# Expert weights read as one run per partition, with strided transposes, in a hybrid backbone step on one core

## Chip, core and metric

One NeuronCore of one Trainium2 chip runs the whole program as a single launch. The metric is the device time of one execution in microseconds. Work is spread over TensorE (PE in the rows, with PEld for its loads of the stationary operand), VectorE (DVE), ScalarE (ACT), GpSimd (POOL) and SyncE (SP). DMAs issued by SP travel on queue q1, those of GpSimd on q0 and those of ScalarE on q10; all run on the same 16 DMA engines.

## What is computed

One layer of a backbone over 512 latent and 128 context tokens of width 1024: a token-mixing half (retention, attention, a diagonal state space), then a mixture of 16 experts. The change touches the experts alone:

```python
logits = (h @ w_router) + b_router            # 16 experts in 4 groups, top 2 inside the best group
hid = silu(einsum('bld,edf->blef', h, w_gate)) * einsum('bld,edf->blef', h, w_up)
out = einsum('blef,efd->bld', hid * combine[..., None], w_down)
```

`w_gate` and `w_up` are 16 matrices of 1024 x 512, `w_down` 16 of 512 x 1024, all float32, so each matrix is 2 MB. An expert computes only on the tokens that chose it.

## The kernel before

The program runs in phases. The last one starts with the output projection and the router (lines 977 to 1036), goes on with the experts (1040 to 1112) and ends with a gather of the expert rows, a sum and a final norm.

**Routing.** The 640 tokens are five tiles of 128 rows, `NROWS[:, t, :]`. VectorE ranks the tokens of each expert and the experts by their number of tokens; GpSimd scatters the rows to the slots of their experts in DRAM (`scratch_x`, line 2657, ten indirect DMAs of 128 rows of 4 KB), in two parts of tiles (tiles 0 to 2, then 3 and 4). The first expert's rows don't go that way: `pick` (1020) multiplies 128 columns of `NROWS` as the stationary operand with a matrix of zeros and ones, which gathers and transposes at once; it makes 40 matmuls, in two parts of 24 and 16.

**Tiles of experts.** There are 13 tiles of 128 slots. Four belong to one expert each (S), nine are in three groups of three where the last 32 slots of each tile belong to a fourth expert. For a tile the steps are `rows` (1040: eight transposes of 128 x 128 from `ROWS2` into PSUM, copied to `COLS`, skipped for tile 0), `gate` and `up` (1072: eight contraction steps of 128 over the 1024 inputs), `turn` (1081: four transposes of `HID`, copied to `HIDT`) and `down` (1089: four contraction steps over the 512 hidden columns, two halves of the output). `MOE_STEPS` writes down the order in which TensorE, VectorE and ScalarE take them. A float32 matmul is two passes on TensorE and a transpose is one, and the rows count passes. In a transpose the data is the stationary operand and the identity matrix moves.

**Weights.** SP brings one 2 MB matrix per DMA in the order of `WEIGHTS` into a ring of seven homes (`load_weights`, 1237, its DMA on line 1244). `home_free` (1246) waits until the matmuls that read the home's last content are done; the home of matrix 6 also waits for the scatter and for the store of `NROWS` in `scratch_h2`. From the fourth matrix on SP needs the expert's number (1266), which VectorE has when the ranks are known. The first three matrices are sent between 852 and 884 us, the next from 975 us on.

**Rows of a tile.** GpSimd waits for all ten scatters, then loads the rows of each tile (512 KB, lines 2682 to 2686) into one of two buffers, as soon as the buffer's last rows are transposed. ScalarE stores each tile's result (512 KB).

With `(k p) c -> p k c` a partition p holds rows p, 128 + p, 256 + p and so on of a matrix: eight runs of 2 KB for `w_gate` and `w_up`, four of 4 KB for `w_down`. The contraction step k then needs inputs 128 k to 128 k + 127, which are neighbouring columns of `ROWS2`, `NROWS` and `HID`.

Of the kernel before, what the change touches and what calls it, by code (L numbers as in the profile page):

```python
# [12 lines left out]
P = 128  # L13
D = 1024
KD = D // P
# [31 lines left out]
def build(nc, a, STOP=99):  # L47
# [6 lines left out]
    def sb(name, shape, dt=F32):  # L54
        return ctx.enter_context(nc.sbuf_tensor(name, shape, dt))

    ident = sb("ident", [P, P])
# [185 lines left out]
    PICK = Region(AQK_AT + 2048).take(NT, P)  # L243
    assert r.at == AQK_AT + 2048 + NT * P
    NROWS_AT = r.at
    NROWS = r.take(NT, D)
# [55 lines left out]
    ROWS2 = r.take(2, D)  # L302
# [4 lines left out]
    HID = r.take(3, 512)  # L307
# [7 lines left out]
    RING = len(W_HOME)  # L315
# [18 lines left out]
    banks = ctx.enter_context(nc.psum_tensor("banks", [P, 8, 512], F32))  # L334
# [54 lines left out]
    slot_in = [sem(f"expert_weights_in{j}") for j in range(RING)]  # L389
# [46 lines left out]
    def at_least(eng, s, n):  # L436

        if not isinstance(n, int) or n > 0:
            eng.wait_ge(s, n)
# [171 lines left out]
    def _(pe):  # L611
# [3 lines left out]
        mm = nc.tensor.matmul  # L615
# [231 lines left out]
        for i, (d, t) in enumerate(KV_ORDER):  # L847
# [4 lines left out]
            for h in range(RH):  # L852
                hs = slice(P * h, P * h + P)
                last = mm(out[:, hs], RK[:, t, hs], VZ[:, i % 3, hs], start=True, stop=True)
            vec.close(last)
        pe.wait_ge(kv_done, len(KV_ORDER))
        for t in range(NT):
            ts_ = slice(P * t, P * t + P)
            out = vec.open(pe)
            for h in range(RH):  # L860
                last = mm(out[:, P * h:P * h + P], RKT[:, h, ts_], RQT[:, h, ts_], start=True, stop=True)
# [5 lines left out]
            for h in range(RH):  # L867
                hs = slice(P * h, P * h + P)
                last = mm(out[:, hs], SS[:, t % 2, hs], RV[:, t, hs], start=True, stop=t == NS)
                if t < NS:  # L870
                    for d in range(2):
                        last = mm(out[:, hs], QX[:, t % 2, d, h, :], ST[:, d, t, hs], start=False, stop=d == 1)
# [83 lines left out]
        for n in range(2):  # L956
            for branch, x in enumerate((ROT, ATT, YT)):
# [3 lines left out]
                for t in range(NT):  # L961
                    for chan, w in list(zip(chans, ws))[::-1]:
                        out = chan.open(pe)
                        for k in range(4):
                            last = mm(out, x[:, k, P * t:P * t + P], w[:, k, :], start=k == 0, stop=k == 3)  # L965
# [55 lines left out]
        def pick(part):  # L1021

            lo, hi = ROUTE_PARTS[part]
            pe.wait_ge(picked, part + 1)
            if part == 0:
                for half in range(2):
                    mm(banks[:, 6 + half, :], PICK[:, NT - 1, :], NROWS[:, 0, 0:512], start=True, stop=False)
            for t in range(lo, hi):
                for k in range(KD):
                    last = mm(banks[:, 6 + k // 4, P * (k % 4):P * (k % 4) + P], NROWS[:, t, P * k:P * k + P], PICK[:, t, :],  # L1030
                              start=False, stop=t == NT - 1 and k % 4 == 3)
            if part:
                last.then_inc(row_t, 1)

        steps = dict(out=project_out, turn=turn_rows, logits=logits, rank=rank, pick=pick)
        for step in OUT_STEPS:
            steps[step[0]](*step[1:])
# [3 lines left out]
        def slot_rows(t):  # L1041
            if t == 0:
                return
            pe.wait_ge(row_in[t % 2], 16 * rows_loaded[t])
            at_least(pe, col_d, t)
            at_least(pe, col_a, t)
            for k in range(KD):
                last = nc.tensor.transpose(banks[:, k // 4, P * (k % 4):P * (k % 4) + P], ROWS2[:, t % 2, P * k:P * k + P], ident[:])
            last.then_inc(row_t, 1)

        def expert_weights(which, t):
# [29 lines left out]
        def slot_turn(t):  # L1081
            n = nth["turn", t]
            pe.wait_ge(gu_free, unit_of["up", t] + 1)
            at_least(pe, hid_c, n)
            for k in range(4):
                last = nc.tensor.transpose(banks[:, 4, P * k:P * k + P], HID[:, t % 3, P * k:P * k + P], ident[:])
            last.then_inc(hid_t, 1)

        def slot_down(t):
# [3 lines left out]
            for half, (full, emptied) in enumerate(((dn0, out_d), (dn1, out_a))):  # L1093
                at_least(pe, emptied, n)
                slot_matmuls(banks[:, 5 + half, :], lambda k: HIDT[:, t % 3, P * k:P * k + P], ws, 4,
                             slice(512 * half, 512 * half + 512)).then_inc(full, 1)

        steps = dict(rows=slot_rows, gate=lambda t: gate_or_up("gate", t), up=lambda t: gate_or_up("up", t), turn=slot_turn, down=slot_down)
        def turn_last():

# [14 lines left out]
        for t in range(NT):  # L1115
# [5 lines left out]
            for half in range(2):  # L1121
                pe.wait_ge(last_gated, half + 1)
                last = mm(banks[:, SPREAD_BANK[t] + half, :], TURNED[:, t, :], GATED[:, 512 * half:512 * half + 512], start=True, stop=True)
# [55 lines left out]
    def _(sp):  # L1179
# [44 lines left out]
        for t in range(NT):  # L1224
            src = a["x_sample"][0, P * t:P * (t + 1), :] if t < NS else a["x_prompt"][0]
# [12 lines left out]
        def load_weights(j, e):  # L1238

            which = WEIGHTS[j][0]  # L1240
            home = (W_DOWN if which == "down" else W_UP)[j % RING]
            src = a[weight_name[which]][0]
            src = src[0] if e is None else src[bass.ds(e, 1)].rearrange("o r c -> (o r) c")
            sp.dma_start(home, src.rearrange("(k p) c -> p k c", p=P)).then_inc(slot_in[j % RING], 16)

        def home_free(j):

# [14 lines left out]
        for j, (which, q, last_tile) in enumerate(WEIGHTS):  # L1262
            if q and q not in numbers:
                if not numbers:
                    sp.wait_ge(routing, ORDERED)
                numbers[q] = sp.value_load(ORDER_E[0:1, q:q + 1], min_val=0, max_val=NE - 1)
            home_free(j)
            load_weights(j, numbers[q] if q else None)
# [1528 lines left out]
```

## Time and profile before

| | us |
|---|---|
| three timed runs | 1325.41, 1321.88, 1320.87 (median 1321.88) |
| the profiled execution, its own time | 1321.03 |
| its span | 1319.4 |
| TensorE busy in the span | 1204.9 (91%) |
| VectorE, ScalarE, GpSimd busy | 546.2, 211.8, 218.5 |
| DMA queue q1 (SP) | 173.52 MB in 80256 packets |
| DMA queue q0 (GpSimd) | 41.01 MB in 14128 packets |

The span runs from the first to the last instruction of the profiled execution; 1.6 us of its own time lie outside. Busy time of an engine counts an interval once, also where pipelined matmuls overlap, so the mean duration of a matmul is longer than the distance between two. A packet of a DMA queue is one contiguous run. The granted clock is given as a share of 2.4 GHz.

### The profile page before, as it was taken

The page shows a single profiled execution, that of the slowest core. Times are in us where ns is not written, and L with a number is a line of the kernel's source. Part 1 is how long each engine was busy: PE and PEld are TensorE (multiplying, and loading weights), DVE is VectorE, ACT ScalarE, POOL GpSimd, SP SyncE. Part 2 cuts the span into 40 slices and gives each one's busy share as a digit, 9 for nine tenths or more (in the row PEclk, how much of TensorE's full clock was granted, in tenths as well). Part 3 has the DMA queues.
Part 4 walks back from the last instruction along what each step waited for, and adds up shares of the span by engine and source line. Part 5 has one row for each costly group of instructions (what it writes and reads, how often), then busy time and mean ns, then how long its engine had stood idle before and what let it go on. Part 6 is the DMA issues. An engine that isn't in the chain of part 4 may idle for free. (4 is left out here: it accounts for less than half of the span.)

```text
span 1319.4 us, 15040 instructions
## 1 busy us (share of the span) xinstructions
PE 1204.9 (91%) x5900; PEld 585.2 (44%) x5900; DVE 546.2 (41%) x1245; ACT 211.8 (16%) x527; POOL 218.5 (17%) x329
## 2 busy tenths in 40 slices
PE   2799799999988999999999999899798998999993
PEld 1445455455755545444444444445453333333331
DVE  2686545848635503333212323325673221121237
ACT  2111012203453322222210000101100000001001
POOL 3008300010069530000000122320030000000020
PEclk9799898999999999999999999989888998999996
DMA  9421502121130162101203466662079999999972
GB/s 299 181 92 37 93 9 84 64 27 38 64 114 21 65 234 117 64 0 64 64 0 128 173 198 224 221 241 107 27 258 361 386 382 361 383 380 382 399 301 82
DMA packets 96191, 221.86 MB, mean 168 GB/s; under 512 B 9385, under 2 KB 11305, under 8 KB 95601
## 3 DMA queue, kind: packets, MB, share of 16 engines
q1 hardware_dynamic: 80256, 173.52, 36.7%
q0 software_dynamic: 14128, 41.01, 10.2%
q10 hardware_dynamic: 1728, 6.29, 1.2%
q8 instruction: 49, 0.80, 0.3%
q14 instruction: 30, 0.24, 0.1%
HBM read 190.32 MB, written 28.38 MB: 166 GB/s over the span
## 5 line engine op out<-in xcount | busy, mean ns | idle before, releaser
L832 PE MATMUL banks<-wring,HT 128*128 128x512 f32 x480 | 216.8, 599 | 0.0
L659 PE MATMUL banks<-wring,HT 128*128 128x512 f32 (+1 forms) x480 | 197.5, 572 | 0.5 <-ACT REG L1356 0.5
L1069 PE MATMUL banks<-REG 128*32 128x512 f32 x1008 | 177.8, 596 | 0.0
L965 PE MATMUL banks<-wring,REG 128*128 128x512 f32 x320 | 139.4, 594 | 1.5 <-DVEq L433 1.5
L659 PEld LDWEIGHTS banks<-wring,HT 128*128 128x128 f32 x480 | 92.5, 195 | 99.3 <-issue 96.1
L832 PEld LDWEIGHTS banks<-wring,HT 128*128 128x128 f32 x480 | 88.1, 191 | 95.9 <-issue 93.5
L965 PEld LDWEIGHTS banks<-wring,REG 128*128 128x128 f32 x320 | 60.1, 190 | 78.2 <-issue 76.2
L1069 PE MATMUL banks<-wring,REG 128*32 128x512 f32 x432 | 81.7, 630 | 2.9 <-DMA REG<-w_gate 2.9
L987 PE MATMUL banks<-wring,REG 128*128 128x512 f32 x160 | 72.9, 614 | 5.6 <-DMA wring<-w_out 5.6
L1069 PEld LDWEIGHTS banks<-REG 128*32 128x32 f32 x1008 | 46.9, 110 | 67.5 <-issue 67.5
L1995 DVE TENSOR_REDUCE REG<-banks 128x1 f32<-128x640 f32 (+1 forms) x40 | 26.8, 712 | 72.5 <-PE banks L906 72.5
L1069 PE MATMUL banks<-HT,REG 128*32 128x512 f32 x288 | 56.4, 593 | 0.0
L987 PEld LDWEIGHTS banks<-wring,REG 128*128 128x128 f32 x160 | 31.0, 197 | 43.2 <-issue 37.3
L635 PE MATMUL banks<-ident,REG 128*128 128x128 f32 x250 | 36.1, 293 | 15.2 <-DVE REG L2088 4.9
L2001 DVE COPY REG<-banks 128x640 f32<-128x640 f32 (+1 forms) x40 | 26.9, 713 | 54.3 <-PE banks L916 54.3
L2275 DVE SCALAR_TENSOR_TENSOR REG<-HT,banks 128x512 f32<-128x512 f32 x13 | 8.9, 687 | 88.5 <-ACT HT L1569 88.4
L1065 PE MATMUL banks<-REG 128*128 128x512 f32 x96 | 42.6, 596 | 1.4 <-ACT REG L1576 1.4
L1427 ACT ACTIVATE REG<-banks 128x512 f32<-128x512 f32 x30 | 17.8, 596 | 158.8 <-PE banks L832 158.8
L635 PEld LDWEIGHTS banks<-ident,REG 128*128 128x128 f32 x250 | 29.7, 150 | 28.5 <-issue 7.6
L2300 DVE TENSOR_TENSOR REG<-banks,REG 128x512 f32<-128x512 f32 x24 | 16.6, 692 | 58.0 <-PE banks L1069 32.6
L1069 PEld LDWEIGHTS banks<-wring,REG 128*32 128x32 f32 x432 | 21.3, 115 | 38.0 <-issue 38.0
L2281 DVE TENSOR_TENSOR REG<-REG,banks 128x512 f32<-128x512 f32 x13 | 8.9, 688 | 68.8 <-PE banks L1069 51.4
(404 smaller groups left out, 1489.7 us busy)
## 6 DMA issues: line engine op xcount, KB each, us to landing
wring<-w_in SPq DMA_DIRECT2D x12, 2048.0 KB, 7.7
REG<-w_down SPq DMA_DIRECT2D x10, 2048.0 KB, 17.9
REG<-w_gate SPq DMA_DIRECT2D x9, 2048.0 KB, 22.6
HT<-w_ada SPq DMA_DIRECT2D x8, 2048.0 KB, 8.2
REG<-w_up SPq DMA_DIRECT2D x8, 2048.0 KB, 19.8
wring<-w_up SPq DMA_DIRECT2D x7, 2048.0 KB, 16.7
scratch_x<-REG POOLq DMA_DIRECT2D x17, 512.0 KB, 10.4
wring<-w_gate SPq DMA_DIRECT2D x4, 2048.0 KB, 17.6
```

The lines of the kernel that those rows point to most:

```text
L635: last = nc.tensor.transpose(out[:, P * j:P * j + P], src, ident[:])
L659: last = mm(out[:, 0:cols], HT[:, k, P * t:P * t + P], w[:, k, 0:cols], start=k == 0, stop=k == KD - 1)
L832: last = mm(chan.bank(), HT[:, k, P * (i % NT):P * (i % NT) + P], gate[1][:, k, :], start=k == 0, stop=k == KD - 1)
L965: last = mm(out, x[:, k, P * t:P * t + P], w[:, k, :], start=k == 0, stop=k == 3)
L987: last = mm(out, MERT[:, k, P * t:P * t + P], out_w[n][1][:, k, :], start=k == 0, stop=k == KD - 1)
L1065: last = mm(out, columns(k), ws[0][:, k, cols], start=k == 0, stop=k == ks - 1)
L1069: last = mm(out[js, :], columns(k)[:, js], ws[j == 3][:, k, cols], start=k == 0, stop=k == ks - 1)
L1427: chan.give(A(TG[GATE_ORDER[i // NT]][:, i % NT, :], src, ACT.Tanh, scale=0.5))
L1995: V_.tensor_reduce(AMAX[:, half:half + 1], flat[:, 1024 * half:1024 * half + P * n], AX.X, ALU.max, negate=True).then_inc(s_max[half], 1)
L2001: cp(PT[half][:, 0:n, P * b:P * b + P], flat[:, 1024 * half:1024 * half + P * n].rearrange("p (c q) -> p c q", c=n)).then_inc(pt_ready[hal ...
L2275: stt(HID[:, t % 3, :], THB[:, n % 2, :], 1.0, banks[:, (2, 3, 7)[u % 3], :], ALU.add, ALU.mult).then_inc(gu_free, 1)
L2300: done(tt(OUT[:, n % 2, ns], banks[:, 5 + half, :], GAIN[:, ns], ALU.mult))
```

## The change

Each partition now holds neighbouring rows: partition p of `w_gate` and `w_up` gets rows 8 p to 8 p + 7, of `w_down` rows 4 p to 4 p + 3. In both cases these are 16 KB in one run. For the sums to stay the same, contraction step k must meet inputs k, k + 8, k + 16 and so on: the transposes of `ROWS2` and the stationary operand of `pick` read every eighth column (32 bytes apart), and those of `HID` every fourth (16 bytes apart). The copies to `COLS` and `HIDT`, the matmuls with the weights, every wait and every order stay as they are. A general path for more tokens than fit the slots keeps its own loads and transposes.

```diff
@@ pick
-                    last = mm(banks[:, 6 + k // 4, P * (k % 4):P * (k % 4) + P], NROWS[:, t, P * k:P * k + P], PICK[:, t, :],
+                    last = mm(banks[:, 6 + k // 4, P * (k % 4):P * (k % 4) + P], NROWS[:, t, k::KD], PICK[:, t, :],
@@ slot_rows
-                last = nc.tensor.transpose(banks[:, k // 4, P * (k % 4):P * (k % 4) + P], ROWS2[:, t % 2, P * k:P * k + P], ident[:])
+                last = nc.tensor.transpose(banks[:, k // 4, P * (k % 4):P * (k % 4) + P], ROWS2[:, t % 2, k::KD], ident[:])
@@ slot_turn
-                last = nc.tensor.transpose(banks[:, 4, P * k:P * k + P], HID[:, t % 3, P * k:P * k + P], ident[:])
+                last = nc.tensor.transpose(banks[:, 4, P * k:P * k + P], HID[:, t % 3, k::4], ident[:])
@@ load_weights
-            sp.dma_start(home, src.rearrange("(k p) c -> p k c", p=P)).then_inc(slot_in[j % RING], 16)
+            sp.dma_start(home, src.rearrange("(p k) c -> p k c", p=P)).then_inc(slot_in[j % RING], 16)
```

No engine gets more, fewer or moved instructions. The one difference in the program's order is the shape of the weight loads on SP, at its first loads of the expert phase (destination, source, then partitions x runs x elements):

```order
-L1244 DMA HT<-w_gate 128x8x512
-L1244 DMA REG<-w_up 128x8x512
-L1244 DMA REG<-w_down 128x4x1024
+L1244 DMA HT<-w_gate 128x4096
+L1244 DMA REG<-w_up 128x4096
+L1244 DMA REG<-w_down 128x4096
```

The eight or four runs of a partition have become one of 4096 float32; the same holds for all 48 weight loads.

## Rows read from the trace of the kernel before

**Rows 1.** The page: busy time by engine, and DMA share in 40 equal slices.
```profile
PE 1204.9 (91%) x5900; PEld 585.2 (44%) x5900; DVE 546.2 (41%) x1245; ACT 211.8 (16%) x527; POOL 218.5 (17%) x329
...
DMA  9421502121130162101203466662079999999972
```

**Rows 2.** Busy time by stretch: stretch, its us, PE, PEld, DVE, ACT, POOL, PEclk, DMA, GB/s.
```profile
975.00:1000.00 25.00, 19.34 (x52) 9.22 (x56) 19.67 (x77) 1.77 (x3) 4.60 (x8) 0.85 1.00 331
1000.00:1290.00 290.00, 282.65 (x2032) 101.08 (x2025) 69.55 (x97) 20.80 (x36) 17.40 (x25) 0.98 1.00 367
```

**Rows 3.** Waits of TensorE from 975 to 1300 us: us in total, times, longest.
```profile
PE banks L1048 <- DMA REG<-scratch_x: 5.6, 2, 3.5
...
PE banks L1069 <- DMA REG<-w_gate: 2.9, 1, 2.9
```

**Rows 4.** TensorE in order of time: start, us, line, operation, count, idle before.
```profile
961.80 5.52 PE L1030 MATMUL banks<-REG 128*128 128x128 f32 x48
967.16 0.31 PE L1014 MATMUL banks<-REG,upper 128*128 128x32 f32 x2
...
994.24 1.09 PE L1048 MATMUL banks<-ident,REG 128*128 128x128 f32 x8 [3.54 <-DMA REG<-scratch_x]
997.42 1.97 PE L1048 MATMUL banks<-ident,REG 128*128 128x128 f32 x8 [2.09 <-DMA REG<-scratch_x]
```

**Rows 5.** Lines 1048, 1086 and 1030 on TensorE: duration ns, min/median/max.
```profile
L1048 PEld LDWEIGHTS banks<-ident,REG x96: 138/141/230, 994.2 to 1256.4; 128*128 128x128 f32 x96
L1048 PE MATMUL banks<-ident,REG x96: 272/273/476, 994.2 to 1256.5; 128*128 128x128 f32 x96
...
L1086 PEld LDWEIGHTS banks<-ident,REG x52: 138/140/143, 1007.9 to 1278.8; 128*128 128x128 f32 x52
...
L1030 PEld LDWEIGHTS banks<-REG x80: 186/192/337, 961.2 to 972.6; 128*128 128x128 f32 x80
```

**Rows 6.** ScalarE, groups by line and form: busy us, mean ns, idle before.
```profile
L1370 ACT ACTIVATE REG<-banks 128x320 f32<-128x320 f32 x8 | 5.3, 761 | 1.2 <-PE banks L806 1.2
...
L1356 ACT ACTIVATE REG<-banks 128x480 f32<-128x480 f32 x4 | 2.1, 570 | 0.0
...
L1356 ACT ACTIVATE REG<-banks 128x320 f32<-128x320 f32 x2 | 0.9, 438 | 0.2
```

**Rows 7.** VectorE in order of time, beside the second `rank`.
```profile
965.14 0.38 DVE L2142 TENSOR_TENSOR REG<-REG 128x16 f32<-128x16 f32 x2
968.16 0.19 DVE L2153 COPY REG<-banks 128x32 f32<-128x32 f32 x1 [2.64 <-PE banks L1018]
```

**Rows 8.** DMA queues from 853 to 855 us: packets, MB, share of 16 engines.
```profile
q0 software_dynamic: 84, 0.69, 81.4%
q1 hardware_dynamic: 84, 0.17, 22.1%
```

**Rows 9.** DMA queue q1, 862 to 866 us, then 892 to 896 us (`w_down`).
```profile
q1 hardware_dynamic: 763, 1.53, 103.0%
...
q1 hardware_dynamic: 337, 1.32, 82.3%
```

**Rows 10.** DMA queues from 992 to 996 us.
```profile
q0 software_dynamic: 214, 0.68, 62.0%
q1 hardware_dynamic: 217, 0.43, 41.2%
```

**Rows 11.** GpSimd in order of time: the last scatter, a store, and the first row load.
```profile
975.17 0.96 POOL L2657 DMA_INDIRECT scratch_x<-REG,sel  x1 [0.31 <-issue]
976.13 0.58 POOL L2649 DMA_DIRECT2D scratch_h<-REG  x1
986.69 0.55 POOL L2684 DMA_DIRECT2D REG<-scratch_x  x1 [9.97 <-DMA scratch_x<-REG,sel]
```

**Rows 12.** SP's DMA issues in order of time, first loads after the ranks are known.
```profile
975.18 2.41 SPq L1244 DMA_DIRECT2D wring<-w_gate  x2
978.83 15.07 SPq L1244 DMA_DIRECT2D REG<-w_gate  x2
```

## The prediction, on record before the changed kernel ran

> **What bounds the kernel now.** I read the page first. TensorE is busy 91% of the span, and the DMA engines, after the start, are full only in the last quarter of it, from about 975 us [rows 1]. The table by stretch shows why they need not matter there: from 1000 to 1290 us the DMA share is 1.00, but TensorE is busy 282.65 of 290 us [rows 2]. Both are full, and the waits say which one ends last. In the whole expert phase TensorE waits for DMA three times: twice for the rows of the first scattered tiles, 5.6 us together, and once for a `w_gate`, 2.9 us [rows 3]. So the stream of weights mostly runs ahead of TensorE, and what a faster stream can give back is of the order of those 8.5 us; anything that lengthens TensorE's own instructions is paid in full.
>
> **Term 1: strided loads of the stationary operand.** The change makes 148 transposes (96 on line 1048, 52 on line 1086) and 80 passes of `pick` (line 1030) read columns 32 or 16 bytes apart; in all of them the data is the stationary operand, so it is PEld that reads with a stride [rows 5]. In a run they follow each other closely: 8 transposes take 1.09 us including a matmul's own 0.27, which makes (1.09 - 0.27) / 7 = 0.117 us a step; 48 passes of `pick` take 5.52, or 0.112 a step [rows 4, 5]. A load lasts 0.14 to 0.19 us [rows 5], longer than the step, so the loads already set the pace, and a slower one lengthens the step.
>
> No strided read by TensorE stands in the trace. Lower bound: nothing, the step stays. A gain is excluded, since no instruction goes. Upper bound, from another engine and from its writing side: line 1370 on ScalarE writes 320 elements 32 bytes apart in 761 ns, where line 1356 writes 320 neighbouring ones in 438; that is 323 ns / 320 = 1.01 ns more an element, or 0.129 us for 128. Neighbouring elements cost (570 - 438) / 160 = 0.825 ns each there, 0.106 us for 128 [rows 6], close to TensorE's step. I take a doubling, + 0.106 us a step, a little under the ratio in the ScalarE rows because reading may do better than writing. In a run of n loads the first is made during the matmul before, so n - 1 count:
>
> - `pick`, first part: 47 x 0.106 = 5.0 us. Nothing covers it: the second `rank` (line 1014) follows it without a wait, while VectorE, done with its inputs at 965.5, waits 2.64 us for it [rows 4, 7]; the scatter's second part and the experts' numbers hang on the rank.
> - `pick`, second part (32 passes): 3.3 us, counted as nothing. It delays `gate` and `up` of tile 0, behind which TensorE waits 3.54 us for rows [rows 4]. Without that wait it costs 3.3.
> - `rows` of 12 tiles: 7 x 0.106 = 0.74 each. The first hides under the wait of the second [rows 4]; 11 x 0.74 = 8.2 us.
> - `turn` of 13 tiles: 3 x 0.106 = 0.32 each, 4.1 us.
>
> Together + 17.3 us, with bounds 0 and 163 x 0.129 (the + 47, + 77 and + 39 steps above) = 21.0.
>
> The ScalarE rows show that 32 bytes between elements cost time [rows 6]; nothing there tells of 16 bytes. The Trainium skill ("SBUF — State Buffer", section "Door 1: The DMA port swizzle") says that SBUF has lines of 16 bytes, that an access which goes to a new line each time pays, and that a stride of 4 float32 is still free. By that rule the four-column stride of `turn` would cost nothing and the sum below would be 4.1 us less; read as two hits per line being needed, it would cost like the rest.
>
> **Term 2: the row loads share the engines with 16 KB runs.** At 853 to 855 us GpSimd's queue moves 8 KB runs and SP's moves 2 KB runs of `w_out`: 84 packets each, so 0.69 MB against 0.17 [rows 8]. The engines alternate by run, not by byte, and q1, which alone moves 1.53 MB in 4 us = 383 GB/s [rows 9], was left 85 GB/s. Between 992 and 996 us, with 4 KB rows against 2 KB weights, it is again 214 packets to 217, and the rows get the larger share: 0.68 MB, 170 GB/s [rows 10]. With weights in runs of 16 KB the ratio of four of rows 8 holds with the roles changed: the rows get about 85 GB/s.
>
> This bites where TensorE already waits. At 975 us SP starts to send weights [rows 12] while GpSimd's last scatter, the store of `scratch_h2` behind it and then the rows of two tiles have to go through, four times 0.52 MB = 2.1 MB [rows 11]. At 85 GB/s that takes 24.7 us. Before, the flow against the weights ended at about 996.3 with the second `rows` starting at 997.42 [rows 4]. If the contention starts when the first weights move, at 978, it now ends at 1002.7 (+ 6.4); if at 981.5, where the flow of q0 starts again after a pause, at 1006.2 (+ 9.9). I take the middle, + 8.2 us. SP's next weight waits for the same scatter, but three matrices (6.3 MB) are in flight by then, so q1 doesn't run dry; the later row loads are issued 10 us and more ahead and are covered. Bounds: 0 (the hardware cuts a run, or shares by byte) and 9.9.
>
> The rows show one run for one run [rows 8, 10]. The Trainium skill ("DMA: Bandwidth & Descriptors", section "Queues, rings and completion order") has an engine drain a whole packet, typically 9 to 17 descriptors, from one queue before it turns to the next. By that the weights' turns would already be some 16 KB, and term 2 would be nothing; equal counts speak against it. That would be the time of the second rival.
>
> **Term 3: the stream.** Runs of 2 KB flow at 383 GB/s; with runs of 4 KB the engines move more per unit of share (1.32 MB at 82.3% for 4 us, 401 GB/s at full share) [rows 9]. So the stream gains about 5%, covered by TensorE except in the 2.9 us wait for `w_gate` [rows 3]. I take all of it: - 2.9 us; bounds 0 and - 2.9.
>
> **Sum.** 17.3 + 8.2 - 2.9 = + 22.6 us on the profiled execution's 1321.03, or 1343.6; the median of the shown runs is 0.85 above that execution, so I predict **1344 us**. A measurement of this kernel can tell about 0.3%, 4 us, from no change.
>
> **Rivals.**
> - *Loads and rows both slower* (the forecast): 1344, with its own range 1337 to 1353. For it: rows 6 and rows 8. Chance 0.36.
> - *Only the strided loads cost.* Large runs are cut, or the queues share by byte, and the rows keep what they had: 1321.9 + 17.3 - 2.9 = 1336. Against it: equal counts in rows 8. Chance 0.17.
> - *Only the row loads suffer.* TensorE's loads have room for a stride because float32 comes slowly anyway (0.83 to 0.92 ns an element): 1321.9 + 8.2 - 2.9 = 1327. Chance 0.21.
> - *Faster.* One mechanism: neither loads nor shares change, and the 5% faster stream brings rows and weights earlier. The place is 975 to 1000 us and the wait for `w_gate`; over some 20 us of flow it gives about 1 us on the rows, and 2.9 on the weights, at most the 5.6 + 2.9 of rows 3: 1313.4 to 1318, most likely 1317. It decides if a run of eight transposes stays under 1.15 us and the first row loads land within 8 us of their issue. Chance 0.16.
> - *No difference*, the weights' runs being cut as before, or gains and small losses cancelling: 1319 to 1323. Chance 0.10.
>
> **How the numbers follow.** Slower by over 0.3% (above 1325.9): the first two rivals' 0.53 and most of the third, 0.71. Faster: 0.16. Within 0.3%: 0.13, the last case and the low end of the third. The high end of the range is the sum at its upper bounds, 21.0 + 9.9 without a gain, 1352.8; the low end reaches into the fourth case: 1315 to 1353. What is left out on both sides is about 0.15.
>
> **What would show it.** Term 1: loads of 0.21 us and more on lines 1048, 1086 and 1030, eight transposes in 1.8 us instead of 1.09, and `rank` later by 5 us. Loads at 0.14 us would strike the term out. Term 2: waits before the first two `rows` of over 10 us together, row loads that land 11 us and more after their issue, packets of q1 at 16 KB and as many of them as of q0 while both flow. Packets of 2 or 4 KB would strike it out. Term 3: no wait for `w_gate`, and q1 alone above 400 GB/s. The prediction is wrong if TensorE's busy time in the expert phase doesn't grow, or if the time falls below 1315.

## The result, and the profile after

The changed kernel takes 1328.86 us (median of 5 runs, 1327.59 to 1333.54), the kernel before 1321.88 (5 runs): ratio 1.0053, 95% interval [1.003, 1.0076], so slower by 0.5% or 7 us. The direction is the one forecast and the time lies in the range; of the + 22.6 us of the sum a third came. Two executions of over 4000 us, one of the kernel before and one of e1 below, are left out of the ratios.

The profiled execution took 1333.54 us. Its page and its waits, to hold against [rows 1] and [rows 3]:

```profile
PE 1215.5 (91%) x5900; PEld 601.6 (45%) x5900; DVE 547.1 (41%) x1245; ACT 211.6 (16%) x527; POOL 218.9 (16%) x329
...
q1 hardware_dynamic: 45440, 173.52, 35.0%
...
REG<-scratch_x POOLq DMA_DIRECT2D x3, 512.0 KB, 12.5
```

```profile
PE banks L1048 <- DMA REG<-scratch_x: 11.9, 2, 7.5
```

The same 173.52 MB now go in 45440 packets instead of 80256. The waits for the first rows have grown from 5.6 to 11.9 us, the 512 KB row loads land in 12.5 us instead of 7.4, and the `w_gate` wait of [rows 3] has no line any more.

TensorE in order of time (start, us, line, operation, count, idle before), to hold against [rows 4]:

```profile
964.79 11.50 PE L1030 MATMUL banks<-REG 128*128 128x128 f32 x48
976.13 0.31 PE L1014 MATMUL banks<-REG,upper 128*128 128x32 f32 x2
...
978.07 7.92 PE L1030 MATMUL banks<-REG 128*128 128x128 f32 x32 [0.98 <-DVEq L2162]
986.92 7.11 PE L1065 MATMUL banks<-HT,REG 128*128 128x512 f32 x16 [0.94 <-DVE REG L2268]
...
1008.42 1.97 PE L1048 MATMUL banks<-ident,REG 128*128 128x128 f32 x8 [7.53 <-DMA REG<-scratch_x]
1014.77 1.97 PE L1048 MATMUL banks<-ident,REG 128*128 128x128 f32 x8 [4.37 <-DMA REG<-scratch_x]
1016.67 7.91 PE L1069 MATMUL banks<-wring,REG 128*32 128x512 f32 x64
...
1032.92 1.05 PE L1048 MATMUL banks<-ident,REG 128*128 128x128 f32 x8
```

The first part of `pick` takes 11.50 us where it took 5.52. But eight transposes take 1.05, as before: the 1.97 of the first two is the clock at its lower level behind a wait (granted 0.50, which is 1.2 of 2.4 GHz), and the second stood in [rows 4] with 1.97 as well. The three strided lines, min/median/max in ns, beside [rows 5]:

```profile
L1048 PEld LDWEIGHTS banks<-ident,REG x96: 185/192/231, 1008.4 to 1268.6; 128*128 128x128 f32 x96
...
L1086 PEld LDWEIGHTS banks<-ident,REG x52: 196/211/220, 1024.5 to 1291.1; 128*128 128x128 f32 x52
...
L1030 PEld LDWEIGHTS banks<-REG x80: 312/336/341, 963.9 to 985.5; 128*128 128x128 f32 x80
```

All three loads are longer (192 for 141, 211 for 140, 336 for 192 ns). The run of `pick` doubles; those of the transposes grow by less than 0.1 us each (numbers below).

The clock is a rival for the longer `pick`. Busy time while it ran, in the order of [rows 2]:

```profile
964.00:976.00 12.00, 12.00 (x50) 11.48 (x48) 3.60 (x20) 0.00 (x0) 0.28 (x1) 0.87 0.24 96
978.00:986.00 8.00, 7.92 (x32) 7.72 (x32) 4.17 (x17) 0.00 (x0) 4.54 (x5) 0.61 0.51 182
```

The granted clock was 0.87 and 0.61 here, and 1.00 during both parts of `pick` in the kernel before. But in e1 below the first part takes 11.46 us with the clock granted at 1.00, so the length comes from the stride.

The queues from 994 to 998 us, where rows and weights flow together, beside [rows 10]:

```profile
q1 hardware_dynamic: 91, 1.49, 86.9%
q0 software_dynamic: 91, 0.31, 18.9%
```

Again one packet for one packet, now 16 KB against 4 KB (the mean of 3.4 KB on q0 counts some packets of 4 bytes): 19% of the engines for the rows, where they had 62%.

**Where the time lies.** The first `rank` starts anywhere from 936.0 to 943.7 us in the profiles of this study, although nothing ahead of it is changed in any of these kernels. So the profiles are compared by stretches behind it, read from timelines like the one above. Stretch 1 goes from the first `rank` (line 1014) to the second and holds the first part of `pick`. Stretch 2 goes from there to the second `rows` and holds the rest of `pick` and the waits for rows. Stretch 3 goes from there to the first matmuls behind the last tile (12 on line 1123, for the sum of the expert rows). Stretch 4 goes to the execution's own end.

| kernel, one profile each | first rank | 1 | 2 | 3 | 4 | 1 to 4 |
|---|---|---|---|---|---|---|
| before | 940.85 | 26.31 | 30.26 | 289.42 | 34.19 | 380.18 |
| after | 943.64 | 32.49 | 38.64 | 284.39 | 34.38 | 389.90 |
| after, second profile (e11) | 939.06 | 32.11 | 38.68 | 284.71 | 34.04 | 389.54 |
| strided reads only (e1) | 939.03 | 32.05 | 32.76 | 287.65 | 34.77 | 387.23 |
| runs only (e2) | 940.20 | 26.26 | 38.81 | 282.77 | 33.95 | 381.79 |
| strided pick only (e3) | 936.00 | 32.48 | 32.67 | 289.22 | 33.95 | 388.32 |
| strided transposes only (e4) | 942.11 | 26.19 | 30.11 | 293.19 | 34.97 | 384.46 |
| after, in runs of 4 KB (e5) | 941.19 | 32.47 | 32.76 | 287.24 | 34.90 | 387.37 |
| first expert old (e6) | 937.87 | 26.14 | 38.66 | 284.26 | 34.18 | 383.24 |
| the same again (e9) | 938.60 | 26.23 | 39.58 | 287.24 | 35.10 | 388.15 |
| the same again (e10) | 937.23 | 26.18 | 39.46 | 287.27 | 34.83 | 387.74 |
| first five experts old (e7) | 938.50 | 27.66 | 30.16 | 284.19 | 34.45 | 376.46 |
| w_down alone (e12) | 943.65 | 26.09 | 30.25 | 287.64 | 34.08 | 378.06 |

Each row is one execution, and its time can lie several us from the median of its kernel: that of e4 took 1326.57 us where the median of 12 is 1319.57, that of e6 1321.11 where it is 1326.51.

The change costs + 6.0 in stretch 1 and + 8.4 in stretch 2 and gains 4.9 in stretch 3 (means of the two profiles of after): + 9.5 behind the first rank.

### The profile page after: what moved, and what is told of

It reads as the page before. It is cut to its first block and busy times, and to the rows that moved or that the text cites. A ratio compares the mean times of both kernels' runs of the same rounds, so it can differ in the third digit from the quotient of the medians.

```text
span 1331.9 us, 15040 instructions
## 1 busy us (share of the span) xinstructions
PE 1215.5 (91%) x5900; PEld 601.6 (45%) x5900; DVE 547.1 (41%) x1245; ACT 211.6 (16%) x527; POOL 218.9 (16%) x329
## 3 DMA queue, kind: packets, MB, share of 16 engines
q1 hardware_dynamic: 45440, 173.52, 35.0%
## 5 line engine op out<-in xcount | busy, mean ns | idle before, releaser
L659 PE MATMUL banks<-wring,HT 128*128 128x512 f32 (+1 forms) x480 | 194.8, 566 | 0.5 <-ACT REG L1356 0.5
L1069 PE MATMUL banks<-REG 128*32 128x512 f32 x1008 | 175.0, 593 | 0.0
L1069 PE MATMUL banks<-wring,REG 128*32 128x512 f32 x432 | 78.1, 602 | 0.0
L676 PE MATMUL banks<-HT,wring 128*128 128x512 f32 (+1 forms) x128 | 36.4, 442 | 0.5 <-ACT REG L1356 0.5
```

The source lines that it names most:

```text
L659: last = mm(out[:, 0:cols], HT[:, k, P * t:P * t + P], w[:, k, 0:cols], start=k == 0, stop=k == KD - 1)
L676: last = mm(out[:, 0:PROMPT if context else SAMPLE], proj[1][:, k, P * h:P * h + P], HT[:, k, cols], start=k == 0, stop=k == KD - 1)
L1069: last = mm(out[js, :], columns(k)[:, js], ws[j == 3][:, k, cols], start=k == 0, stop=k == ks - 1)
```

## The experiments

After the result theory A was: the strided loads cost in `pick` alone, and the 16 KB runs cost at the first rows what they give back at `w_gate`. Its rivals: B, only the runs cost, and `pick` was slow by its clock; C, only the strides cost, those of the transposes too.

### Each part of the change alone

In these four kernels, where only one side is changed, a contraction step pairs inputs with other rows of the weights than the reference does; the amount of work is the same. e1 makes the three strided reads of the diff and keeps the old load; e2 makes the new load and keeps the old reads.

> The strided reads of the change (pick, rows, turn) with the weights laid out as before, so experts multiply inputs with the wrong rows of their weights. Theory A (strided loads cost in pick alone, 16 KB runs delay the first rows and end the wait for w_gate): pick's first 48 passes about 11.5 us instead of 5.5, loads of pick 0.33 us, eight transposes still about 1.1 us, the wait for w_gate still there: 1328 to 1331 us. Theory B (only the runs matter, pick was slow because TensorE's clock had fallen by chance): 1322. Theory C (only the strided loads matter): 1329, no less than the changed kernel.

> The new layout of the weights alone, all TensorE reads contiguous as before, so experts multiply inputs with the wrong rows of their weights. Theory A: pick at 5.5 us again, the two waits for the first rows 11 to 14 us together instead of 5.6, no wait for w_gate and no matmuls at half clock behind it (about - 6): 1323 to 1326 us. Theory B: the same as the changed kernel, 1329. Theory C: no slower than before, 1316 to 1322.

e3 and e4 split the reads.

```diff
 e3
-  NROWS[:, t, P * k:P * k + P]
+  NROWS[:, t, k::KD]
 e4
-  ROWS2[:, t % 2, P * k:P * k + P]
+  ROWS2[:, t % 2, k::KD]
-  HID[:, t % 3, P * k:P * k + P]
+  HID[:, t % 3, k::4]
```

> Strided reads in pick alone, everything else as before, so the first expert's columns come in another order than its weights. Theory A: + 6 us for the first 48 passes, the second 32 passes mostly hidden under the wait for rows: 1327 to 1330 us. Theory B: 1322. Theory C: with the transposes' part missing, 1327.

> Strided reads in the transposes of rows and turn alone, everything else as before, so experts multiply inputs with the wrong rows of their weights. Theory A: loads 0.19 and 0.21 us instead of 0.14, but eight transposes within 0.1 us of before and four 0.09 us longer, 13 x 0.09 + 12 x 0.04 = 1.7 us: 1322 to 1325. Theory B: 1322. The recorded prediction's term of 12.3 us for them would give 1334.

Measured against the kernel before on the same chip (1321.45 us): e1 1330.17, ratio 1.0057 [1.0038, 1.0076]; e2 1321.96, 1.001 [0.9991, 1.003]; e3 1327.76, 1.0057 [1.0037, 1.0076]; e4 1319.57, 0.9992 [0.9971, 1.0013]. The strided `pick` alone gives the same ratio as all strided reads, and within the intervals that of the whole change. Its timeline (e3), then that of the runs alone (e2):

```profile
957.14 11.50 PE L1030 MATMUL banks<-REG 128*128 128x128 f32 x48
...
968.48 0.31 PE L1014 MATMUL banks<-REG,upper 128*128 128x32 f32 x2
...
970.42 7.89 PE L1030 MATMUL banks<-REG 128*128 128x128 f32 x32 [0.98 <-DVEq L2162]
...
1001.15 1.94 PE L1048 MATMUL banks<-ident,REG 128*128 128x128 f32 x8 [3.81 <-DVE REG L2268]
```

```profile
961.10 5.52 PE L1030 MATMUL banks<-REG 128*128 128x128 f32 x48
966.46 0.31 PE L1014 MATMUL banks<-REG,upper 128*128 128x32 f32 x2
...
999.05 1.97 PE L1048 MATMUL banks<-ident,REG 128*128 128x128 f32 x8 [9.04 <-DMA REG<-scratch_x]
1005.27 1.97 PE L1048 MATMUL banks<-ident,REG 128*128 128x128 f32 x8 [4.25 <-DMA REG<-scratch_x]
```

In e3, 957.14 to 968.48 is 11.3 us to the second `rank`, where e2 has 5.4 as before. In e2 the waits for rows are 13.3 us; by the table it loses 8.6 in stretch 2 and gains 6.7 in stretch 3. In e3 and e1 the second part of `pick` takes 4.1 us longer too, and with rows that are not delayed stretch 2 is 2.4 to 2.5 us over the kernel before. Where the rows are late anyway, stretch 2 is 38.7 with the strided `pick` (after) and 38.8 without (e2): the second part is hidden.

B falls: e1 and e3 are slower without any run of 16 KB. The times of e1 to e3 don't part A from C, which foresaw that of e2 better (1316 to 1322, where A had 1323 to 1326). Against C stand e4, where by the interval the strided transposes cost at most 0.13% or 1.7 us (A had it at 1322 to 1325, also too high), and the trace of e2, where the runs alone delay the rows and end the `w_gate` wait. Each part of A is thus seen in a trace. Whether loss and gain of the runs cancel was to be seen below.

### What the length of a run does

The changed kernel, each matrix as four transfers with runs of 4 KB (64 counts a load instead of 16):

```diff
-  sp.dma_start(home, src.rearrange("(p k) c -> p k c", p=P)).then_inc(slot_in[j % RING], 16)
+  rows_of = src.rearrange("(p k) c -> p k c", p=P)
+  n = rows_of.shape[1] // 4
+  for i in range(4):
+      sp.dma_start(home[:, n * i:n * i + n], rows_of[:, n * i:n * i + n]).then_inc(slot_in[j % RING], 16)
```

> The changed kernel with each weight matrix sent as four transfers whose runs are 4 KB, not 16 KB, with the same layout and the same strided reads. Theory A (the engines take the two queues run for run, so a flow gets its share by the length of its runs): the rows (4 KB) get half of the engines instead of a fifth, as between 992 and 996 us of the kernel before; the waits for the first rows fall from 11.9 to 6 to 9 us, a row load lands in 8 to 9 us instead of 12.5, the pick stays at 11.5 us; time 3 to 5 us under the changed kernel, 1324 to 1326. Rival (the share doesn't hang on the run; the rows are late because the pick is): waits near 12 and the time of the changed kernel, 1329.

1323.97 us against 1320.06 before on that chip, ratio 1.0027 [1.0008, 1.0047]. Its DMA queues from 988 to 992 us, and its row loads from the page:

```profile
q0 software_dynamic: 226, 0.86, 52.4%
q1 hardware_dynamic: 227, 0.83, 50.5%
```

```profile
REG<-scratch_x POOLq DMA_DIRECT2D x3, 512.0 KB, 7.8
```

One packet for one again, and at equal lengths half of the engines for the rows, whose loads land in 7.8 us instead of 12.5. Stretch 2 falls from 38.7 to 32.76, exactly where e1 has it with 2 KB runs and the same strided `pick`. So the run against which a row load competes sets its delay, and 6 us of stretch 2 hang on it. The time alone would not show this: the intervals of this ratio and of the changed kernel's overlap. The second `rows` there waits 4.46 us for VectorE (line 2271 there, 2268 in the kernel before), no longer for a DMA.

### Two versions between

e6 keeps the first expert's gate and up in the old layout, so that `pick` reads neighbouring columns; everything else is as changed. e7 keeps the first five experts' gate and up old, and the rows' transposes of the first four tiles. In both, and in e9 and e10, line numbers are one higher.

```diff
+OLD = (0,)                # e7: (0, 4, 5, 6, 7)
-  NROWS[:, t, k::KD]
+  NROWS[:, t, P * k:P * k + P]
-  "(p k) c -> p k c"
+  "(k p) c -> p k c" if which != "down" and q in OLD else "(p k) c -> p k c"
 e7 only
-  ROWS2[:, t % 2, k::KD]
+  ROWS2[:, t % 2, P * k:P * k + P] if t < 4 else ROWS2[:, t % 2, k::KD]
```

> The changed kernel, but gate and up of the first expert alone come in the old layout (2 KB runs), so that the pick can read neighbouring columns; all later weights, and the transposes, as changed. Theory A (the pick is the whole net loss): first pick back at 5.5 us, loads of L1030 at 0.19; the waits for the first rows stay at 11 to 13 us, since later weights in 16 KB runs flow beside them; no wait for w_gate; time as with the new runs alone plus up to 1.7 for the strided transposes, 1320 to 1324. Rival (the transposes cost too): 1328 or more.

> As the run before it, but the gate and up of the first five experts come in the old layout, 2 KB runs, and the first four tiles' rows are transposed from neighbouring columns; w_down from the start, and everything from the sixth expert on, as changed. If the rows are late because 16 KB runs flow beside them, and the w_gate wait ends because 4 to 16 KB runs flow faster later, both gains can be had: waits for the first rows 5 to 8 us, no wait for w_gate over 1 us, time 1315 to 1319, under the kernel before. Rival (the two go together: weights that come earlier take from the rows whatever their runs): the waits' sum stays at 10 or more, time 1320 to 1323.

e7 takes 1318.72 us against 1320.06, ratio 0.9982 [0.9971, 0.9993]: faster than both kernels, if by 0.2%, and at the high end of what was expected. Its waits, and its first gate behind the second `rows`:

```profile
PE banks L1049 <- DMA REG<-scratch_x: 6.3, 2, 5.3
```

```profile
993.31 1.97 PE L1049 MATMUL banks<-ident,REG 128*128 128x128 f32 x8 [5.30 <-DMA REG<-scratch_x]
996.32 1.97 PE L1049 MATMUL banks<-ident,REG 128*128 128x128 f32 x8 [1.04 <-DMA REG<-scratch_x]
998.21 7.74 PE L1070 MATMUL banks<-wring,REG 128*32 128x512 f32 x64
```

Early rows and a stream without a `w_gate` wait can be had together: stretch 2 is that of the kernel before, stretch 3 is 5.2 us under it (0.9 of this is the clock in the first gate, 7.74 us for 8.65).

e6 missed: 1326.51 us, ratio 1.0042 [1.0023, 1.0061], with times in two groups. Two more profiles of it were taken, with one of the changed kernel, and beside them the smallest version that the table suggests: the new layout for `w_down` alone, with the strided `turn` that it needs.

> The kernel with the first expert's gate and up in the old layout, once more, for a second profile: its times lay in two groups, 1320 to 1323 and 1326 to 1331, and the one profile is of the first. Theory A (the pick is the only part of the change that costs; the second group comes of TensorE's clock in code ahead of the change, which starts earlier or later): from the start of rank's first part (L1015) to the end again 383 us within 2, whatever the total, and in a total of 1326 or more that rank starts at 941 or later instead of 937.9. Rival (the long wait for the first rows lets the clock fall, and for longer in some executions): rank starts near 938 and the 6 us more lie behind 995 us, in gate, up and down groups at half clock.

> The same kernel and the same question as in the run before it, for a third profile: rank's first part to the end 383 us within 2 by theory A; 386 or more in a total of 1326 by the rival.

> The changed kernel itself, for a second profile and more times beside the others on one chip. Theory A: rank's first part to the end about 388 to 390 us as in its first profile (389.9, against 380.2 before), also where that rank starts earlier than 943.6; pick 11.5 and 7.9 us again; median 1326 to 1330, ratio 1.004 to 1.007. Rival (its first profile was disturbed behind the rank): 385 or less there, median 1325 or less.

```diff
 e12, against the kernel before
-  HID[:, t % 3, P * k:P * k + P]
+  HID[:, t % 3, k::4]
-  "(p k) c -> p k c"
+  "(p k) c -> p k c" if which == "down" else "(k p) c -> p k c"
```

> The new layout for w_down alone (16 KB runs instead of 4 KB) with turn's strided transposes; gate and up, the pick and the rows' transposes as in the kernel before. If the gain behind the first tiles is the faster stream of all weights, this keeps a part of it: w_gate waits under 2.9 us but not gone, time 1317 to 1321. If w_down's runs delay the rows as the others do: waits for the first rows 8 us or more instead of 5.6, time 1320 to 1324. If only the runs of gate and up matter, nothing changes: waits 5.6 and 2.9, the time of the kernel before.

e9 (1326.75 us) and e10 (1324.97) decide for the rival as to the place: 388.15 and 387.74 us behind the first rank instead of 383.24, with that rank as early as in e6. The timeline of e9, at its first gate and at the last tile's `down`:

```profile
1004.41 1.97 PE L1049 MATMUL banks<-ident,REG 128*128 128x128 f32 x8 [4.73 <-DMA REG<-scratch_x]
1006.31 9.07 PE L1070 MATMUL banks<-wring,REG 128*32 128x512 f32 x64
...
1282.98 8.83 PE L1066 MATMUL banks<-REG 128*128 128x512 f32 x16 [0.69 <-ACT REG L1577]
```

The first gate takes 9.07 us for 7.79 in e6, and the last `down` 8.83 for 7.13: two places where the clock was at its lower level for longer (granted 0.83 from 1280 to 1290 us here, 1.00 in e6). Together 3.0 us, the whole difference in stretch 3 between e6 and e9; stretches 2 and 4 are 0.9 longer each. The rival's cause is not shown: behind waits for rows of 13.3 us the first gate takes 7.77 us in e2, and behind shorter ones 9.11 in e5. The same 8.83 stands in the profiles of e4, e5 and e10 too, some 280 us behind the waits for rows. Why these two groups find the lower level in some executions is open.

With the two groups set aside, stretch 3 is 269.30 to 269.35 us in all seven profiles with strided transposes and no `w_gate` wait (after, e5, e6, e7, e9, e10, e11), 267.87 in e2 and 273.64 in the kernel before. So there the strided transposes cost 1.5 us and the end of the wait gives 5.8. Stretches 1 to 3, counted in this way against the kernel before, are + 10.3 and + 9.9 in the changed kernel, + 7.4 in e1, + 2.7 in e2, + 8.4 in e3, + 1.8 in e4, + 4.3 in e5, + 3.9 in e6, - 3.1 in e7 and - 1.9 in e12. All ten lie within the intervals of the measured ratios or less than 0.3 us outside. Without the strided `pick` the change thus still loses some 4 us (5.5 in the times of e6): theory A was wrong to call `pick` the whole net loss.

e11: 1329.52 us against 1323.29, ratio 1.0065 [1.0042, 1.0088]; the table has its stretches beside those of the first profile, and they agree. e12: 1320.27 us, ratio 0.9986 [0.9968, 1.0003], not told apart from the kernel before; in its profile the first waits stay at 5.6 and that for `w_gate` falls from 2.9 to 1.1:

```profile
PE banks L1048 <- DMA REG<-scratch_x: 5.6, 2, 3.7
...
PE banks L1069 <- DMA REG<-w_gate: 1.1, 1, 1.1
```

### Strides by themselves

The kernel before with extra work in the expert phase: 12 matmuls (two passes each) with the stationary operand read at a stride of 1, 2, 4 and 8 elements (lines 1089 to 1095), and 24 transposes at each stride (1097 to 1103).

```diff
+  for k in range(12 if t == 4 else 0):
+      mm(to(k), at(k, 8), ident[:], start=True, stop=True)
...
+  for k in range(24 if t == 8 else 0):
+      nc.tensor.transpose(to(k), at(k, 8), ident[:])
```

> The kernel before with extra work on TensorE in the expert phase, each variant on a line of its own and in one tile: 12 two-pass float32 matmuls whose stationary operand is read with a stride of 1, 2, 4 or 8 elements (L1089, L1091, L1093, L1095), then 24 transposes with each of these strides (L1097, L1099, L1101, L1103); they write a bank that is then overwritten, so the outputs stay. Theory A (a strided load is longer, and shows only where it outlasts the pass beside it): matmul loads 0.19 us at stride 1 and about 0.33 at stride 8, with the step of a pass going from 0.11 to over 0.2; transposes' loads 0.14 at stride 1, about 0.2 at strides 4 and 8, their step at most 0.13. Open: where between 1 and 8 the matmul's loads grow. Rival (16 bytes between elements is free): stride 4 like stride 1 in both. Time about 10 us over the kernel before.

Each line's loads, strides 1, 2, 4 and 8, first of the matmuls and then of the transposes; the two times behind the durations are the first and the last start:

```profile
L1089 PEld LDWEIGHTS banks<-ident,REG x24: 186/192/193, 1042.0 to 1044.5; 128*128 128x128 f32 x24
...
L1091 PEld LDWEIGHTS banks<-ident,REG x24: 195/196/197, 1052.3 to 1055.0; 128*128 128x128 f32 x24
...
L1093 PEld LDWEIGHTS banks<-ident,REG x24: 308/329/330, 1062.7 to 1068.1; 128*128 128x128 f32 x24
...
L1095 PEld LDWEIGHTS banks<-ident,REG x24: 312/335/337, 1108.3 to 1113.7; 128*128 128x128 f32 x24
...
L1097 PEld LDWEIGHTS banks<-ident,REG x24: 138/140/143, 1150.9 to 1153.4; 128*128 128x128 f32 x24
...
L1099 PEld LDWEIGHTS banks<-ident,REG x24: 197/209/216, 1161.1 to 1163.8; 128*128 128x128 f32 x24
...
L1101 PEld LDWEIGHTS banks<-ident,REG x24: 196/209/219, 1171.6 to 1174.4; 128*128 128x128 f32 x24
...
L1103 PEld LDWEIGHTS banks<-ident,REG x24: 185/193/207, 1212.9 to 1215.4; 128*128 128x128 f32 x24
```

A matmul's pass goes from one to the next in 2.5 / 23 = 0.109 us at stride 1, 0.117 at 2, and 5.4 / 23 = 0.235 at 4 and 8 alike. A transpose's step is 0.109, 0.117, 0.122 and 0.109, though its load is 38 to 49% longer at every stride over 1. The clock was granted at 1.00 in all eight runs. The rival, 16 bytes free in both, falls. The time, 1340.57 us, missed: I expected + 10 and it is + 20, where the eight runs last 30 us in sum; how much of them lies beside other work was not followed up.

## Why the prediction was right or wrong

**Term 1, pick: right, a little small.** Forecast + 5.0 for the first part, measured 11.50 - 5.52 = 5.98. The doubling of the step was the right pick between the bounds: 0.127 us more a step where 0.106 was taken, close to the upper bound of 0.129 from [rows 6]. That a price from ScalarE's writes fits TensorE's reads is luck as far as the runs show: it was a price for 32 bytes between elements, and TensorE's matmuls pay the same at 16. The second part was counted as nothing, since TensorE waits for rows behind it. It is 4.1 us longer; after and e2 show it hidden, and in e1 and e3, where the rows come early, stretch 2 is 2.4 to 2.5 longer.

**Term 1, rows and turn: the step that failed.** The prediction said that loads of 0.14 us, longer than the step of 0.117, "already set the pace, and a slower one lengthens the step", and put 8.2 + 4.1 = 12.3 us on it. The loads did grow, to the "0.21 us and more" on lines 1086 and 1030 by which the text meant to recognise the term, and to 0.19 on line 1048. The other half of that sign, eight transposes in 1.8 us, did not come: they take 1.05 or 1.16 us for 1.04 to 1.09, and four transposes of `turn` 0.75 for 0.66. Busy us and mean ns of all transposes, in the kernel before and then in e4, where only they are strided:

```profile
L1048 PE MATMUL banks<-ident,REG 128*128 128x128 f32 x96 | 13.6, 288 | 5.6 <-DMA REG<-scratch_x 5.6
...
L1086 PE MATMUL banks<-ident,REG 128*128 128x128 f32 x52 | 8.5, 286 | 0.9 <-DVE REG L2281 0.9
```

```profile
L1048 PE MATMUL banks<-ident,REG 128*128 128x128 f32 x96 | 13.9, 291 | 5.4 <-DMA REG<-scratch_x 5.4
...
L1086 PE MATMUL banks<-ident,REG 128*128 128x128 f32 x52 | 9.7, 310 | 0.9 <-DVE REG L2281 0.9
```

That is + 0.3 and + 1.2, together 1.5 us, and the table agrees (269.34 in stretch 3 without the two groups, against 267.87 in e2). A transpose's load of 0.14 or 0.21 us beside a step of 0.11 to 0.12 shows that the record's length is not the interval between loads. The price from ScalarE held for a two-pass matmul and was carried over to a transpose, where it does not hold. Why a transpose's longer load does not lengthen its step, no run shows. This one error of 10.8 us is most of the 13.1 by which the sum of 22.6 lies over the + 9.5 of the stretches.

The Trainium skill ("SBUF — State Buffer", section "Door 1: The DMA port swizzle") has a stride of 4 float32 as free. For `turn` the time comes out close to that, though its loads do not (211 ns for 140); for a two-pass matmul it does not hold (329 ns at stride 4 against 196 at stride 2, and the step doubles). The rule would have made the sum 4.1 us less, for a reason that the loads do not bear out.

**Term 2: right.** Forecast + 8.2 from a packet-for-packet share; stretch 2 grew by 8.4, with 91 packets to 91, and e5 turns it off by the run's length. That it came so close is luck, since 8.2 was the middle between + 6.4 and + 9.9. The order of the packets shows the alternation itself. Set end to start, those of the changed kernel from 994 to 998 us make 16 chains, as many as there are engines, and in 165 of 166 successions the queue changes; a weight packet of 16 KB takes 611 ns and a row packet of 4 KB 159. The Trainium skill ("DMA: Bandwidth & Descriptors", section "Queues, rings and completion order"), by which an engine drains some 9 to 17 descriptors of a queue in turn, would have made the term nothing as the prediction read it; these chains speak against such turns for this pair of queues.

**Term 3: too small.** Forecast - 2.9, the wait. In stretch 3 e2 gains 6.7. Of this 0.9 lies in the first gate (7.77 us for 8.65), which is the clock and not the stream. The other 5.8 are twice the wait, because the clock fell behind it. TensorE's stretch from 1080 to 1100 us and the next, with the granted clock behind the busy time, in the kernel before (the wait ends at 1095.8) and in e2:

```profile
1080.00:1100.00 20.00, 16.29 (x64) 0.87 1.05 375
1100.00:1120.00 20.00, 19.31 (x124) 0.96 1.01 357
```

```profile
1080.00:1100.00 20.00, 19.17 (x85) 1.00 1.02 389
1100.00:1120.00 20.00, 19.31 (x132) 1.00 1.00 384
```

20 x 0.13 + 20 x 0.04 = 3.4 us of clock lie around that wait and go with it. In steps of 5 us the order is seen: granted 1.00 up to 1090, 0.97 while TensorE waits, 0.50 from 1095 to 1100, 0.85 to 1105. The wait of 2.7 us in e4 and that of 1.1 in e12 are followed by a low clock too (0.57 and 0.71 from 1095 to 1100), but one of 2.7 us in e1 (up to 1193) is not: granted 1.00 there. The term's 5% is a slip that the sum does not use: it sets 383 GB/s at a share of 103% beside 401 at full share, and at equal share [rows 9] give 372 and 401, or 8%.

**The sum as measured.** 6.0 + 8.4 + 1.5 - 5.8 and - 0.6 in the first gate (8.65 us before, 7.91 and 8.24 in the two profiles of after) is + 9.5, what the stretches gave; the two comparisons of times gave + 7 and + 8.6 (0.65% of 1323.29), with intervals of 3 us to either side. The rival nearest in time, "only the row loads suffer" at 1327, had the transposes right and the `pick` wrong; it came near because the gain of the stream, 3 us larger than it said, makes up for half of the 6 us that it lacks.

## What to carry to other kernels

Price a slower operand by the step of the run that it is in, for each kind of instruction apart: a load that lasts longer in the trace need not come more rarely. When two DMA queues share the engines run for run, long runs in the bulk stream are paid by the short runs beside it; make them long only where nothing urgent flows, as e7 did. And a wait of TensorE that goes away can take the low clock behind it along, in the kernel before as much again as the wait itself.

## What the runs showed of the hardware that I had not expected

- A float32 matmul of two passes loads its stationary operand as fast at a stride of 8 bytes as at none (196 and 192 ns) and in 329 to 336 ns at 16 and 32 bytes, with the step of a pass doubled. Transposes load in 193 to 209 ns at any stride from 8 to 32 bytes, not monotonic, with the step hardly changed.
- The one-for-one alternation of two queues holds for runs of 16 KB (91 to 91) as for 4 KB (226 to 227), and at 16 KB it is seen packet by packet (165 of 166 successions).
- One kernel's profiles differ by 5 us behind the same start (383.24, 388.15, 387.74), of which 3.0 lie in two groups of 64 and 16 matmuls that found the clock at its lower level.
